# Folding squared pairs on VectorE ahead of a ones-sum, and another order of bank copies and slab splits, in a two-block transformer kernel

## The reference, cut to what matters

```python
def rms_norm_2(x, g):
    y = x32 * lax.rsqrt(jnp.mean(x32 * x32, axis=-1, keepdims=True) + EPS)
    return (y * g.astype(jnp.float32)).astype(x.dtype)

def per_layer_embedding(h, p_i, w_gate, w_proj, post_norm):
    return rms_norm_2(jax.nn.sigmoid(h @ w_gate) * (p_i @ w_proj), post_norm)

x = first_block(...)          # ends with conv_ffn and rms_norm(h, norm_final)
for i in range(DEPTH_2):      # 2 layers
    x = x + 0.5 * swiglu(...)
    x = x + m                                              # even_mixer or mla_mixer
    x = x + 0.5 * swiglu(...)
    x = x + per_layer_embedding(rms_norm_2(x, g[3]), p[i], ple_w_gate[i], ple_w_proj[i], g[4])
```

## Time and profile before

| | |
|---|---|
| Median of 3 runs | 1674.85 us (1674.37 to 1675.96) |
| The profiled execution | 1679.27 us, its span 1677.3 us |
| PE busy / weight loads busy | 1635.7 us (98%) / 1498.1 us (89%) |
| DVE busy / ACT busy | 1240.6 us (74%) / 923.8 us (55%) |
| PE's share of the chain that ended last | 83% |
| Mean granted clock of PE | 0.995 |

### The profile page before, as it was taken

The page is one execution under the profiler, slowest core; times in us unless marked ns, Lnnn a source line. Parts: engine busy times, 40 slices in busy tenths (PEclk is TensorE's granted clock), DMA queues, the critical chain, the costliest instruction groups (busy, mean ns, idle before and its releaser), DMA issues.

```text
span 1677.3 us, 29553 instructions
## 1 busy us (share of the span) xinstructions
PE 1635.7 (98%) x12590; PEld 1498.1 (89%) x12590; DVE 1240.6 (74%) x1358; ACT 923.8 (55%) x1016; POOL 39.7 (2%) x40
## 2 busy tenths in 40 slices
PE   8999998999999999999999999999999999999997
PEld 8988898999999998888999888888888897988887
DVE  6777777975788888776697687657877578777655
ACT  5376434544665567554576555438555456565445
POOL 0000000100000000000030000000000000000000
PEclk9999999999999999999999999999999999999999
DMA  8524445453454544555633455463555542455551
GB/s 297 186 88 164 159 146 197 153 206 120 157 201 175 203 172 154 201 191 189 213 128 125 160 200 200 163 208 131 201 195 170 187 177 75 155 179 193 188 182 57
DMA packets 84136, 287.14 MB, mean 171 GB/s; under 512 B 5856, under 2 KB 54112, under 8 KB 56384
## 3 DMA queue, kind: packets, MB, share of 16 engines
q1 hardware_dynamic: 79984, 273.70, 46.6%
q0 software_dynamic: 2816, 10.69, 1.8%
q10 hardware_dynamic: 1232, 1.25, 0.2%
HBM read 281.42 MB, written 4.19 MB: 170 GB/s over the span
## 4 chain that ended last, share of the span: by engine, by line
PE 83%; DVE 10%; ACT 3%; issue 2%; DMA 1%; POOL 0%; ACTq 0%; DVEq 0%; POOLq 0%
PE PS L476 83%; DVE ring_lo L2146 3%; DVE arena L2149 2%; DVE arena L2146 2%; ACT ring_hi L1484 1%; ACT arena L1484 1%; DVE operand L2211 1%; DMA arena<-spilled_gates 1%; DMA arena<-in_ple_t 0%; DVE residual L2146 0%; ACT L1484 0%; DVE inv L2205 0%; DVE arena L2306 0%; DMA residual<-in_x_t 0%; ACT operand L1484 0%
## 5 line engine op out<-in xcount | busy, mean ns | idle before, releaser
L476 PE MATMUL PS<-operand,ring_hi 128*128 128x256 f32 (+1 forms) x4360 | 909.0, 330 | 16.0 <-DVE operand L2211 10.2
L476 PEld LDWEIGHTS PS<-operand,ring_hi 128*128 128x128 f32 x4360 | 728.5, 191 | 84.8 <-issue 10.6
L2146 DVE TENSOR_TENSOR ring_lo<-ring_raw,ring_hi 128x2048 fp32r<-128x2048 f32 (+2 forms) x267 | 600.3, 2250 | 211.1 <-ACT ring_hi L1484 210.8
L1484 ACT ACTIVATE ring_hi<-ring_raw 128x2048 fp32r<-128x2048 f32 (+2 forms) x267 | 497.1, 1863 | 194.3 <-PE PS L476 179.5
L476 PE MATMUL PS<-operand,ring_lo 128*128 128x256 f32 x3060 | 601.1, 283 | 0.0
L476 PEld LDWEIGHTS PS<-operand,ring_lo 128*128 128x128 f32 x3060 | 480.3, 192 | 11.8
L1484 ACT ACTIVATE arena<-PS 128x512 f32<-128x512 f32 (+2 forms) x141 | 89.6, 641 | 173.1 <-PE PS L476 163.1
L476 PE MATMUL PS<-hidden,ring_hi 128*128 128x512 f32 x704 | 174.8, 396 | 0.0
L476 PEld LDWEIGHTS PS<-hidden,ring_hi 128*128 128x128 f32 x704 | 128.0, 188 | 26.1
L1484 ACT ACTIVATE arena<-arena 128x512 f32<-128x512 f32 (+6 forms) x124 | 85.4, 703 | 68.8 <-DVE arena L2149 41.0
L2146 DVE TENSOR_TENSOR arena<-arena,PS 128x512 f32<-128x512 f32 (+4 forms) x147 | 99.6, 682 | 28.6 <-ACT arena L1484 21.6
(11 more groups left out here) (160 smaller groups left out, 1128.7 us busy)
## 6 DMA issues: line engine op xcount, KB each, us to landing
ring_raw<-in_w_stream SPq DMA_DIRECT2D x215, 1024.0 KB, 4.8
ring_raw<-in_w_stream SPq DMA_DIRECT2D x64, 512.0 KB, 4.4
ring_raw<-in_w_stream SPq DMA_DIRECT2D x52, 256.0 KB, 3.4
spilled_gates<-arena POOLq DMA_DIRECT2D x12, 256.0 KB, 3.0
arena<-spilled_gates POOLq DMA_DIRECT2D x2, 1536.0 KB, 10.3
tables<-in_tables POOLq DMA_DIRECT2D x1, 1344.0 KB, 9.4
residual<-in_x_t ACTq DMA_DIRECT2D x4, 256.0 KB, 7.8
arena<-in_mem_t POOLq DMA_DIRECT2D x1, 1024.0 KB, 16.9
```

Of the source, the lines that this page charges most:

```text
L476: return nc.tensor.matmul(out, lhs, rhs, start=start, stop=stop, skip_group_check=True)
L1484: return nc.scalar.activation(out, in_, func, **kw)
L2146: return v.tensor_tensor(out, a, b, op)
```

## The change

The change has five parts.

1. DVE adds the two squared tiles of chunks 0, 1 and 2 (`fold_squares`, 128x256), and PE has one ones-call for each of them and two for the last chunk: five calls in place of eight, at A, B and C. At A the three adds stand between the residual adds of `conv_down`. At B and C two stand ahead of `gate_scale(2)` and one behind `gate_product(3)`.
2. At B, all of `embed(1)` stands behind the sums. Before, two of its eight column blocks stood ahead of the last chunk's sums.
3. In `per_layer` of ACT, `split_slab(g0 + 5)` moves ahead of `squared(2)`, and `gained(2)` behind `squared(3)`.
4. Of `embedding_out`, the copy of bank 2 stands behind the last operands of the norm and ahead of the last square. The other three copies move into `feed_forward`, behind `up(0)`. PE waits for them only ahead of the down product.
5. At B, ACT's split of slab 1 of `ffn_2` (`START["ple_0"] + 6`) moves from ahead of chunk 2 to behind the last operands, between the copy of bank 2 and the last square.

Two semaphores (`sb_exp`, `ca_exp`) are also merged into one, which adds no instruction and no wait.

```diff
             def sums_and_embedding(n, b, squared, done):
-                for c in range(4):
-                    if c == 3 and n == 1:
-                        pe.wait_ge(lo_split, START[f"emb_{n}"] + 1)
-                        embed(n, range(2))
-                    pe.wait_ge(sem("chunk_squared"), squared + c + 1)
-                    if c < 3 or b == 3:
-                        last = chunk_sums(b, 2 * c, c == 0, c == 3)
...
+                for c in range(3):
+                    pe.wait_ge(sem("chunk_folded"), 3 * n + c + 1)
+                    mm(bank(b)[:, 0:T], table("ones"), squares[:, 2 * c, :], c == 0, False)
+                for i in range(2):
+                    pe.wait_ge(sem("chunk_squared"), squared + 4 + (i if b == 0 else 0))
+                    last = mm(bank(b)[:, 0:T], table("ones"), squares[:, 6 + i, :], False, i == 1)
                 last.then_inc(sem(done), 1)
...
                 if embedded is not None:
-                    pe.wait_ge(sem("ple_copied"), embedded + 1)
+                    pe.wait_ge(sem("ple_copied"), 4 * embedded + 1)
...
+                if embedded is not None:
+                    pe.wait_ge(sem("ple_copied"), 4 * embedded + 4)
...
                     operand_tiles((2 * c, 2 * c + 1), H, gain, 0)
+                    if c == 3 and last is not None:
+                        last()
                     square(c)
...
                 gate(0)
                 up(0)
+                if embedded is not None:
+                    embedding_out(embedded, 1, 4)
...
-            chunks("final", ("norm_gains", 0))
-            embedding_out(0)
-            feed_forward("ffn_0")
+            chunks("final", ("norm_gains", 0), last=lambda: embedding_out(0, 0, 1))
+            feed_forward("ffn_0", embedded=0)
...
                 gated(2, slice(4, 6))
+                split_slab(g0 + 5)
                 squared(2, slice(4, 6))
-                gained(2)
-                split_slab(g0 + 5)
                 gated(3, slice(6, 7))
                 squared(3, slice(6, 7))
+                gained(2)
...
-            chunks("ple_0", ("norm_gains", 40), (None, None, START["ple_0"] + 6))
-            embedding_out(1)
-            feed_forward("ffn_2")
+            chunks("ple_0", ("norm_gains", 40), last=lambda: (embedding_out(1, 0, 1), split_slab(START["ple_0"] + 6)))
+            feed_forward("ffn_2", embedded=1)
...
+            def fold_squares(n, c):
+
+                dve.wait_ge(sem("chunk_squared"), 5 * n - (n > 0) + c + 1)
+                tt_(squares[:, 2 * c, :], squares[:, 2 * c, :], squares[:, 2 * c + 1, :], ALU.add)\
+                    .then_inc(sem("chunk_folded"), 1)
...
                     tt_(chunk(c), chunk(c), bank(4 + c), ALU.add).then_inc(sem("residual_ready"), 1)
+                    if c:
+                        fold_squares(0, c - 1)
...
                 split_slab(g0 + 4)
+                fold_squares(n + 1, 0)
+                fold_squares(n + 1, 1)
                 gate_scale(2)
...
                     gate_product(3 + m, slice(6 + m, 7 + m))
+                    if m == 0:
+                        fold_squares(n + 1, 2)
```

More of the change, by code:

```diff
@@ L577, in sums_and_embedding @@
             def sums_and_embedding(n, b, squared, done):
-                for c in range(4):
-                    if c == 3 and n == 1:
-                        pe.wait_ge(lo_split, START[f"emb_{n}"] + 1)
-                        embed(n, range(2))
-                    pe.wait_ge(sem("chunk_squared"), squared + c + 1)
-                    if c < 3 or b == 3:
-                        last = chunk_sums(b, 2 * c, c == 0, c == 3)
[L587 to L590, removed]
-                last.then_inc(sem(done), 1)
[L592 to L597, removed]
+                for c in range(3):
[4 more added lines that the diff above has]
+                    last = mm(bank(b)[:, 0:T], table("ones"), squares[:, 6 + i, :], False, i == 1)
+                last.then_inc(sem(done), 1)
+                if n < 2:
+                    if n == 0:
+                        operands(1)
+                    pe.wait_ge(lo_split, START[f"emb_{n}"] + 1)
+                    embed(n, range(KT))
             def operands(n):
@@ L653, in norm_sum @@
                 last.then_inc(sem("norm_summed"), 1)
-            def chunk_sums(b, k, start, stop):
-                mm(bank(b)[:, 0:T], table("ones"), squares[:, k, :], start, False)
-                return mm(bank(b)[:, 0:T], table("ones"), squares[:, k + 1, :], False, stop)
             ffns = [0]
@@ L1514, in square, with chunks @@
                     .then_inc(sem("norm_squared"), 1)
-            def chunks(stage, gain, slabs=()):
+            def chunks(stage, gain, slabs=(), last=None):
                 for c in range(4):
@@ L1628, in conv_feed_forward, with feed_forward @@
                 ffns[0] += 1
-            def feed_forward(name, root_first=False):
+            def feed_forward(name, root_first=False, embedded=None):
                 g0, n = START[name], ffns[0]
@@ L1751, in attention @@
                 act.wait_ge(sem("sb_logw"), q + 1)
-                run(sb_w[q], sb_w[q], ACT.Exp).then_inc(sem("sb_exp"), 1)
+                run(sb_w[q], sb_w[q], ACT.Exp).then_inc(sem("probs_raised"), 1)
             def shift(j):
@@ L1880, in _ @@
                                bias=small[:, 8 + i:9 + i], accum_out=small[:, 16 + i:17 + i])
-                last.then_inc(sem("ca_exp"), 1)
+                last.then_inc(sem("probs_raised"), 1)
             split_slab(START["ca_o"])
@@ L1894, in embedding, with embedding_out @@
                 operand(XH[:, 8:10], ple_in)
-            def embedding_out(n):
+            def embedding_out(n, first, end):
                 act.wait_ge(multiplied, START[f"emb_{n}"] + 1)
-                for i, b in enumerate(EMB_BANKS):
-                    last_ = run(flat(embedded[:, 2 * i:2 * i + 2]), bank(b))
-                last_.then_inc(sem("ple_copied"), 1)
+                for i in range(first, end):
+                    run(flat(embedded[:, 2 * i:2 * i + 2]), bank(EMB_BANKS[i])).then_inc(sem("ple_copied"), 1)
             conv_feed_forward("ffn_c")
@@ L2526, in attention @@
                 tt_(sb_w[q], sb_w[q], bank(3, 3), ALU.add).then_inc(sem("sb_logw"), 1)
-                dve.wait_ge(sem("sb_exp"), q + 1)
+                dve.wait_ge(sem("probs_raised"), q + 1)
                 masked(q, sb_w[q]).then_inc(sem("sb_att"), 1)
@@ L2820, in _ @@
             for tt in range(2):
-                dve.wait_ge(sem("ca_exp"), tt + 1)
+                dve.wait_ge(sem("probs_raised"), tt + 3)
                 r = small[:, 24 + 4 * tt:28 + 4 * tt]
@@ L3003, in per_layer @@
                 norm_factor()
-                dve.wait_ge(sem("ple_copied"), n + 1)
+                dve.wait_ge(sem("ple_copied"), 4 * n + 4)
                 def gate_product(part, tiles):
```

## The result

The changed kernel took 1680.33 us (median of 13 runs, 1678.28 to 1682.99), beside 1675.41 us for the kernel before (13 runs): ratio 1.0032, 95% interval 1.0024 to 1.0040. That is slower by 5.4 us (4.0 to 6.7), where +2.9 was forecast, and outside the range. The profiled pair differs by only 1.7 us (1680.96 and 1679.27). So the three places have to be read one by one.

A forecast was written before the change was run, and what follows sets the result against it. PE was taken as the bound, its waits hanging on an ACT and DVE chain. Terms +1.16 at A, +2.07 at B, -0.34 at C gave +2.9 us on 1674.85: 1677.7, range 1675.2 to 1679.6.

The forecast's parts named there:

- A, earlier Ln and what follows, at `norm_sum`: Sums among `conv_down`'s residual adds, ahead of `ffn_0`: Ln starts 0.27 us earlier, and `norm_sum` with it.
- A, three copies behind `up(0)`: In `ffn_0`: three bank copies on ACT delay slab 4 on PE by 1.43 us, nothing hiding it.
- B, Ln: Sums ahead of `ffn_2`: Ln starts at 1155.88 in place of 1156.85, a gain of 0.97 us.
- B, `norm_sum` behind the late split: In `ffn_2`: ACT's later split of slab 1 holds DVE, so `norm_sum` starts 0.64 us later despite the earlier Ln.
- B, three copies: In `ffn_2`: three bank copies behind `up(0)` on ACT delay slab 4 on PE by 1.43 us.
- C, Ln: Last of the three sums, no slab split there: Ln starts 0.34 us earlier, a gain lasting to the program's end.
- the clock's rival: PE's clock falls in longer waits at `norm_sum` or ahead of slab 4; once gives +4.4 us, 1679.3; chance 0.17.
- Rival 4: PE's clock falls in longer waits at `norm_sum` or ahead of slab 4: 1679.3 us once, 1680.8 twice; chance 0.17.
- a drop behind `norm_sum` would in part vanish: In `ffn_2`: time lost to a clock drop behind `norm_sum` would partly disappear in the wait ahead of slab 4.
- The price of 1.5 us: Cost forecast for one fall of PE's clock behind a longer wait: 4 us at 0.62 cost 1.5 us.
- Rivals 1 to 3: 1: copies hidden, 1674.9 us (0.11); 2: only earlier Ln counts, 1673.3 (0.04); 3: Ln start floor 1.65 us, 1678.9 (0.03).
- The second rival: Only the earlier Ln counts at the three sums; slab 1's split would not hold DVE: -1.6 us, 1673.3; chance 0.04.

## Why the prediction missed

| step | forecast | measured by place |
|---|---|---|
| A, earlier Ln and what follows, at `norm_sum` | -0.27 | -0.18 |
| A, three copies behind `up(0)` | +1.43 | +1.47 |
| B, Ln | -0.97 | -0.97 |
| B, `norm_sum` behind the late split | +0.64 | +0.66 |
| B, three copies | +1.43 | +1.55, 0.11 to 0.15 of it the clock |
| C, Ln | -0.34 | -0.35 |
| sum | +2.9 | +3.15 |

The row "B, Ln" is contained in the row below it and not added again. The measured values come from the distances: at A `norm_sum` is at 19.54 us from the mark before and 19.36 after, at B the Ln at 190.76 and 189.79, and `norm_sum` at 206.29 and 206.95. At A the Ln itself came 0.28 us sooner, and 0.10 of it was lost on the way to `norm_sum`. PE's wait at `norm_sum` at B was 2.49 us and not "about 2.2". In the prediction's working of the late split the parts that it names add up to 1168.28 and not 1168.33, which is 0.05 us of the +0.64.

**What failed is the step from the sum to the time: "1674.85 + 2.9 = 1677.7", with a range whose upper end came from the clock's rival alone.** It put the scatter of both medians at nothing, though the prediction itself says that a measurement can't tell 3.3 us from no change. The base was the median of 3 runs; the 88 runs of the three later sets of the same kernel have a median of 1675.86, 1.0 us higher. And two medians of the changed kernel differ by 3.4 us. Over all its runs the changed kernel has a median of 1679.13, inside the range; the first set's 1680.33 was not. Some 1.0 us of the miss of 2.6 is the base, 0.25 the terms, and the other 1.3 or 1.4 the scatter of that set, in part its clock of 0.9941 against the 0.9951 and 0.9955 of the two others. Why that set had the lower clock stays open; no trace shows that the change has a part in it.

**Rival 4 happened and did not decide.** The clock did fall behind the wait at `norm_sum`, in three of the four profiles of that wait left unfilled. It cost 0.11 to 0.15 us and not 1.5, since PE stood 1.7 us before slab 4 anyway. The sentence "a drop behind `norm_sum` would in part vanish" was right, and should have gone further: nearly all of it vanishes. The price of 1.5 us is not wrong as such: the profiles with a second fall between slab 4 of `ffn_2` and the last table load are 1.1 to 1.9 us longer there. Behind the 1.7 us ahead of slab 4 the clock never fell.

**Rivals 1 to 3.** The copies are not hidden (1.46 us for three, each time). The Ln does start right behind its load, 1.29 to 1.31 us after the load began, in all three places, so the floor is 1.3 and not 1.65. The Trainium skill, "ScalarE: Activation LUTs", section "What ACT_TABLE_LOAD costs", gives the 1.28 us that the trace shows, and about as much again for a drain behind the load, which no row here shows. The second rival's -1.6 is what came out once parts 4 and 5 were undone: -1.51 by place.

## What to carry to other kernels

Before work is moved behind an instruction, follow that queue to the next thing PE waits for: three copies of 0.48 us behind `up(0)` cost their full 1.46, twice, and ate the gain of the folds, while ahead of slab 2 they had been free. A wait of PE that is followed by a second wait for another engine's queue is free up to the size of the second, and so is a fallen clock between the two. When the effect looked for is smaller than the scatter, compare distances between marks of one profile, close around the edit. At A and B they repeated within 0.02 us for the same kernel, while a distance of some 305 us that the change doesn't touch spread by 2.9 us (303.24 to 306.18). And allow for the scatter of both medians in the range.

## What was not expected of the hardware

More than half of the variance of a kernel's runs goes with their mean granted clock (1.38 us for each 0.001). At the same instruction, after the same wait of 2.48 us, the clock fell in three profiles and not in a fourth. No fall followed the one wait of 1.51 us at that place or the nine of 1.7 us ahead of slab 4.
